# A hybrid decoder layer on one core: the output projection by token halves, the sample rows kept by channel through both norms, and the second norm's sums taken from accumulator outputs

## The reference, cut to what matters

```python
mix = (sigmoid(gate_pool) * A + sigmoid(gate_rwkv) * B) @ w_out
x  = LN1(ALPHA * x + (1 + gate1(c)) * mix)
h2 = LN0(x) * (1 + scale2(c)) + shift2(c)
ff = ConvFFN(h2)     # up-projection, causal conv of width 3, SiLU gate, down-projection
x  = LN2(ALPHA * x + (1 + gate2(c)) * ff)
```

## Time and profile before

| | |
|---|---|
| median of 3 runs | 1205.17 us (1204.91 to 1206.76) |
| the profiled execution | 1207.57 us, of it 1205.8 us from the first to the last instruction |
| PE busy | 1109.9 us, 92% |
| DVE, ACT, POOL busy | 58%, 40%, 8% |
| granted TensorE clock, mean | 0.977 of full |

### The profile page before, as it was taken

The page is one execution under the profiler, slowest core; times in us unless marked ns, Lnnn a source line. Parts: engine busy times, 40 slices in busy tenths (PEclk is TensorE's granted clock), DMA queues, the critical chain, the costliest instruction groups (busy, mean ns, idle before and its releaser), DMA issues.

```text
span 1205.8 us, 34828 instructions
## 1 busy us (share of the span) xinstructions
PE 1109.9 (92%) x15398; PEld 1028.4 (85%) x15398; DVE 705.3 (58%) x1141; ACT 484.5 (40%) x804; POOL 100.7 (8%) x152
## 2 busy tenths in 40 slices
PE   4789999999999999999989997799999989599995
PEld 2678888888888878999989997798999989599995
DVE  5456666677666663679316538756666576723336
ACT  2375344363443633543324233554443444413221
POOL 0003203032030310000000003100000000000000
PEclk9899999999999999999989999899999999899998
DMA  9502202102021102397775522322323223242221
GB/s 322 184 25 58 60 4 60 45 19 61 3 61 46 54 18 58 96 266 214 220 226 175 159 88 71 106 71 70 104 70 91 83 75 99 84 149 80 84 69 71
DMA packets 188225, 117.50 MB, mean 97 GB/s; under 512 B 6693, under 2 KB 180379, under 8 KB 187954
## 3 DMA queue, kind: packets, MB, share of 16 engines
q1 hardware_dynamic: 157333, 100.17, 27.7%
q10 hardware_dynamic: 30764, 15.40, 4.6%
HBM read 108.40 MB, written 7.34 MB: 96 GB/s over the span
## 4 chain that ended last, share of the span: by engine, by line
PE 30%; issue 8%; DVE 8%; ACT 7%; DMA 3%; SPq 1%; POOL 1%; DVEq 1%; ACTq 0%; POOLq 0%
PE PJ L231 22%; PE PJ L223 4%; ACT ACC L1938 2%; ACT Wh L1744 2%; DVE ACC L2338 2%; DVE ACC L2339 1%; DMA AD<-in_ada_w_dram 1%; DVE ACC L2346 1%; DVE ACC L2344 1%; ACT ACC L1936 1%; PE BB L1513 1%; DMA RAW<-in_w_in_dram 1%; DVE Wl L1988 1%; PE BB L231 1%; ACT SFh L1945 0%
## 5 line engine op out<-in xcount | busy, mean ns | idle before, releaser
L231 PE MATMUL PJ<-Hh,Wh 128*128 128x260 f32 (+1 forms) x1152 | 257.9, 305 | 20.2 <-DVE Wl L1988 13.6
L231 PE MATMUL PJ<-Hl,Wh 128*128 128x260 f32 (+1 forms) x1152 | 234.3, 285 | 0.0
L231 PE MATMUL PJ<-Hh,Wl 128*128 128x260 f32 (+1 forms) x1152 | 233.5, 284 | 0.0
L231 PEld LDWEIGHTS PJ<-Hh,Wh 128*128 128x128 f32 x1152 | 179.4, 190 | 43.5 <-issue 32.1
L1988 DVE TENSOR_TENSOR Wl<-RAW,Wh 128x1024 fp32r<-128x1024 f32 (+2 forms) x102 | 118.2, 1161 | 110.8 <-ACT Wh L1744 105.6
L231 PEld LDWEIGHTS PJ<-Hh,Wl 128*128 128x128 f32 x1152 | 180.0, 190 | 0.0
L231 PEld LDWEIGHTS PJ<-Hl,Wh 128*128 128x128 f32 x1152 | 179.6, 190 | 0.0
L1744 ACT ACTIVATE Wh<-RAW 128x1024 fp32r<-128x1024 f32 (+2 forms) x106 | 106.8, 1010 | 118.3 <-PE PJ L231 114.4
L2338 DVE SCALAR_TENSOR_TENSOR ACC<-ACC,CP 128x512 f32<-128x512 f32 x88 | 66.1, 751 | 72.7 <-ACT ACC L1938 71.1
L1304 POOL TENSOR_TENSOR MO<-BP,CST 128x512 f32<-128x512 f32 x40 | 55.9, 1405 | 309.4 <-DVE KP L1185 250.1
L231 PE MATMUL PJ<-SFh,Wh 128*128 128x256 f32 (+1 forms) x308 | 64.3, 290 | 13.4 <-DVE Wl L1988 13.4
(11 more groups left out here) (389 smaller groups left out, 2153.5 us busy)
## 6 DMA issues: line engine op xcount, KB each, us to landing
RAW<-in_w_in_dram SPq DMA_DIRECT2D x46, 512.0 KB, 5.3
RAW<-in_ffn_up_dram SPq DMA_DIRECT2D x44, 512.0 KB, 3.8
AD<-in_ada_w_dram ACTq DMA_DIRECT2D x19, 512.0 KB, 5.8
RAW<-in_ffn_down_dram SPq DMA_DIRECT2D x16, 512.0 KB, 3.9
RAW<-in_ada_w_dram ACTq DMA_DIRECT2D x10, 512.0 KB, 6.6
AW<-in_ada_w_dram SPq DMA_DIRECT2D x2, 2048.0 KB, 14.6
RAW<-in_w_branch_rwkv_dram SPq DMA_DIRECT2D x8, 512.0 KB, 4.1
RAW<-in_w_out_dram SPq DMA_DIRECT2D x8, 512.0 KB, 4.0
```

The source lines that it names most:

```text
L231: mm = pe.matmul(out[:, b, 0:nb[b]], w[:, slot, kw, :], x[:, kx, c0:c0 + nb[b]], start=first and w is Wh and x is xh, stop=last and w is Wl)
```

## The change

- **w_out by halves.** All eight blocks go by halves. First pass: tokens 256 to 519 of blocks 0 to 7 (`ohalf`, with `wt(e)` for the place of the split weights: blocks 4 to 7 lie in parts of `Hh` and `Hl`, so all eight stay). Second pass: tokens 0 to 255 in the order 4, 5, 0, 1, 2, 3, 6, 7. Tiles 2 and 3 are turned, added and normed during the second pass, turned back in it (`turn_x`), and the up-projection's first half is now tokens 256 to 519. Tiles 0 and 1 are normed during that.
- **Samples by channel.** The 8 sample columns are never turned to rows for a norm. They stay a 128x64 array (`XT_`, `GX`); `x_sample` is turned once to channels by PE; a norm's sums over channels are a `tensor_reduce` over the blocks on DVE and a small product with a matrix of 1/1024 on PE (`total`, `total2`), the root is ACT's (`root_s`). The weights and biases of both norms are loaded a second time by channel (four small loads on ACT's queue at the start). Only at the end PE turns the samples to rows for the output, and ACT copies them.
- **Sums from accumulators.** `stats_x` is gone. `finish_x` is `finish` with an accumulator output (the sum of the row); the mean's negative is one 128x1 operation; `root_x` is a `Square` over 128x1024 on ACT with an accumulator output and then the root.
- **No POOL between w_out and the up-projection.** The low parts of the four weight blocks and of `Hl` are made by DVE.
- **The end.** The last down block does tokens 256 to 519 first; tiles 2 and 3 are normed and stored before tiles 0 and 1. The sample rows' statistics, centring and finish are gone from DVE.

PE's queue, cut:

```diff
-                for e in range(NF):
+                for e in range(KT):
                     pe.wait_ge(S("w_lo"), B_OUT + e + 1)
+                    after(pe, "mo1", e - 1)
                     after(pe, "mo1_s", e - 1)
...
-                        mm = kstep(pe, PJ[e % 2], e % 4, k, MGh, MGl, k, k == 0, k == KT - 1, nh)
+                        mm = ohalf(PJ[e % 2][:, 0, 0:264], e, k, 256, 264)
+                    mm.then_inc(S("half"), 1)
+                    if e > 1 and e % 2 == 0:
+                        turn(e // 2 - 1, (e - 2, e - 1), (2, 3))
...
+                for p, e in enumerate(E2):
+                    after(pe, "mo1", KT + p - 1 if p > 1 else 0)
+                    for k in range(KT):
+                        if p == 0 and k == 3:
+                            turn(3, (6, 7), (2, 3))
+                        mm = ohalf(PJ[e % 2][:, 1, 0:256], e, k, 0, 256)
                     mm.then_inc(S("prj"), 1)
+                    if p == 0:
+                        total(0, 2)
+                    elif p == 1:
+                        total(1, 3)
+                    elif p == 2:
+                        turn(4, (4, 5), (0, 1))
+                    elif p == 3:
+                        total(2, 4)
+                    elif p == 4:
+                        turn(5, (0, 1), (0, 1))
+                        past(pe, "xn", 2)
...
+                        for b in range(3):
+                            turn_x(HA[b], b, (2, 3), b)
+                    elif p == 5:
+                        past(pe, "hfd", 1)
+                        turn_x(HA[3], 3, (2, 3), 3)
+                        total(3, 5)
+                    elif p == 6:
+                        turn(6, (2, 3), (0, 1))
+                turn(7, (6, 7), (0, 1))
```

DVE's and ACT's new norm steps, and POOL's part:

```diff
+                def finish_x(t, n):
+                    dve.scalar_tensor_tensor(x_row(t), x_row(t), RS1[:, t:t + 1], LNP[:, 1, :], ALU.mult, ALU.add,
+                                             accum_out=MVX[:, t, 0:1]).then_inc(S("x1"), 1)
+                    dve.wait_ge(S("x1"), n)
+                    dve.tensor_scalar(MVX[:, t, 1:2], MVX[:, t, 0:1], -1.0 / D, None, ALU.mult).then_inc(S("mv"), 1)
+                def s_centre(dst, mean, left, sq):
+                    dve.wait_ge(S("t_y"), left)
+                    need(mark(dve.tensor_tensor(dst, XT_, by_b(mean), ALU.subtract)))
+                    need(mark(dve.tensor_tensor(sq, dst, dst, ALU.mult)))
+                    dve.tensor_reduce(RED, over_k(sq), AX.X, ALU.add).then_inc(S("ys"), 1)
...
-                def root_x(t, n):
+                def root_x(t, n, left):
                     past(act, "mv", n)
+                    act.activation(xn_row(t), x_row(t), ACT.Square, bias=MVX[:, t, 1:2], accum_out=RS2[:, t:t + 1]).then_inc(S("sd"), 1)
+                    past(act, "sd", left)
+                    act.activation(RS2[:, t:t + 1], RS2[:, t:t + 1], ACT.Sqrt, bias=CST[:, C_EPS:C_EPS + 1], scale=1.0 / D).then_inc(S("sd"), 1)
...
-                for q in range(4):
-                    pool.wait_ge(S("w_hi"), B_FF + q + 1)
-                    pool.wait_ge(S("w_lo"), B_FF + q)
-                    pool.tensor_tensor(Wl[:, q], RAW[:, q], Wh[:, q].bitcast(F32), ALU.subtract).then_inc(S("w_lo"), 1)
-                for b in range(4):
-                    past(pool, "hh", b + 1)
-                    pool.tensor_tensor(Hl[:, 2 * b:2 * b + 2, 0:256], HR[:, 2 * (b % 2):2 * (b % 2) + 2, :],
-                                       Hh[:, 2 * b:2 * b + 2, 0:256].bitcast(F32), ALU.subtract).then_inc(S("hl_a"), 1)
```

More of the change, by code:

```diff
@@ L1878, in _ @@
+                gated1(0)
+                root(2, 4, 1)
+                gated1(1)
+                root_s(sums(1), 4)
+                root_x(2, 2, 2)
+                gated1(2)
+                normed(2, 1)
                 split_ff(0)
-                gated1(NF + 1)
+                root_x(3, 3, 4)
+                gated1(3)
+                normed(3, 2)
                 split_ff(1)
-                root_x(0, 2)
-                gated1(NF + 2)
+                gated1(4)
+                half_f(0, HA, 1)
@@ L1891, in _ @@
-                for b in range(4):
-                    after(act, "hl_a", b - 1)
-                    half_f(b, HA, b + 1)
-                    past(act, "hf", b + 1)
-                    half_h(b, 0)
-                    if b == 1:
-                        root(2, 5, 4)
-                root_x(2, 5)
-                normed(2, 3)
-                root_x(3, 6)
-                normed(3, 4)
-                root_x(4, 7)
+                act.wait_ge(S("hl_a"), 1)
+                half_f(2, HA, 3)
@@ L1903, in _ @@
+                past(act, "hf", 2)
+                half_h(2, 256)
+                gated1(6)
+                past(act, "hfd", 2)
+                act.activation(Hh[:, :, T:TN], HS, ACT.Copy).then_inc(S("hh"), 1)
+                past(act, "hfd", 3)
+                half_h(3, 256)
+                gated1(7)
+                root(0, 2, 4)
+                root_x(0, 5, 7)
+                normed(0, 3)
+                root_x(1, 6, 9)
+                normed(1, 4)
                 act.wait_ge(S("hl_a"), 3)
@@ new lines, in _ @@
+                dve.wait_ge(S("xa"), 4)
+                need(mark(chunk((2, 3), 3, x_row)))
+                joined((2, 3))
+                past(dve, "ld_c", 32)
+                past(dve, "mv", 1)
+                s_centre(XT_, sums(0), 3, GX)
+                c2 = centre(x_row, LNP, 2)
+                inverse(2, 4, 1)
+                need(c2)
+                finish_x(2, 1)
+                c3 = centre(x_row, LNP, 3)
+                inverse_x(2, 3)
+                need(c3)
+                finish_x(3, 2)
@@ new lines, in _ @@
+                joined((0, 1))
+                past(dve, "mv", 4)
+                c0 = centre(x_row, LNP, 0)
+                inverse(0, 2, 6)
+                need(c0)
+                finish_x(0, 3)
+                c1 = centre(x_row, LNP, 1)
+                inverse_x(0, 8)
+                need(c1)
+                finish_x(1, 4)
+                inverse_x(1, 10)
+                dve.wait_ge(S("hl_a"), 4)
+                half_f(1, HB, 6)
+                half_l(0, 6, 0, "hl_b")
+                half_l(1, 7, 0, "hl_b")
@@ L2365, in _, with add2 @@
                 J = TURNS1
-                def add2(e, tiles, sample):
-                    j = J + (e if e < KT - 1 or not sample else KT)
-                    add(j, XP2, XS2, tiles, e, 1, sample, B[2])
+                def add2(e, tiles):
+                    add(J + (e if e < KT - 1 or tiles[0] else KT), XP2, tiles, e, 1)
                 def lo_dn(e, q):
```

562 lines of the change are left out of this document (273 added, 289 removed).

## The result

The changed kernel takes 1185.59 us (median of 4 runs, 1183.3 to 1186.1), the kernel before beside it 1205.04 (4 runs, 1201.1 to 1206.76). The ratio is 0.9836, with a 95% interval of 0.9817 to 0.9855: 1.6% faster. The prediction said 1187.2 us, 1184 to 1194.5. The profiled execution took 1183.3 us, 1181.5 of it from the first to the last instruction.

The account below looks back on a forecast made before the run. PE, busy 92%, bounds the kernel; time comes only from its stops and low clock. `w_out` to loop: 76.8 work, 4.9 waits, 0.4 allowance, 82.1. Gains 16.0 + 0.7 + 1.3 = 18.0 give 1189.6 profiled, median 1187.2 us, range 1184 to 1194.5.

Parts of the forecast that it names:

- Work at full clock, 76.8: PE's work from `w_out` to the up-projection loop, in us: products, turns, sample transposes, sums, `XN` transposes, first four up blocks.
- First block, 0.9: First `w_out` block: a new PE wait of 0.9 us for the low part of `MGl` for `k = 7`.
- Tiles 2 and 3: no wait, margin 0.8: Second `w_out` pass: normed rows ready at 736.1 us, PE reaches them at 736.9; no wait.
- Tiles 0 and 1: a wait of 0.9: After the first up halves: PE ends at 760.3 us, `xn` 4 comes at 761.2, so PE waits 0.9.
- Accumulators, 0.2 each: Norm sums by accumulator output: 0.2 us each; rival: `finish_x` takes 1.2 more each, 1190.7 us, 10%.
- Second half, 1.3 and 1.0: Up blocks' second half: PE waits 1.3 us after transposing `XN`, then 1.0 for the third pair of blocks of `h2`.
- POOL's 7.6 us hidden: POOL's splits become 7.6 us of DVE work, covered by the second `w_out` pass; uncovered they would cost 7.6 us.
- The loads hidden: First loop weights: loads go at 758.6 us, ACT wants the first at 769.9, 3 us left; cost nothing.
- Down, 0.7 gained; last add 0.9 later: Down-projection: seven small transposes leave PE, 0.7 us gained; samples by channel move DVE's last add from 1193.5 to 1194.4.
- The end: After the last add: 3.4 us of sample work leaves DVE, last store lands about a microsecond later; 1.3 gained, 0.3 to 2.5.
- The low clock: Rival: clock falls again at PE's three waits between 760.3 and 768 us, costing 3 us; 1190.2 us, 17%.
- the slower rival's mechanism: DVE's 128x1 steps slow behind any large pass, not through POOL; 12 at 1.9 us each give 1210 us; 4%.

Follow-up runs that it names:

- The order that avoids it: Changed kernel with the last k of the first `w_out` block done after three k of the second block: 1185.85 us, ratio 0.9857; stretch 81.62.
- 2.2 in one piece, made on purpose: Changed kernel with six needless `bn_stats` ahead of the statistics of tiles 0 and 1: 1190.93 us, ratio 0.9885; stretch 85.40.
- the changed kernel again: Changed kernel run once more, unaltered, for a second profile: 1186.37 us, ratio 0.9853; stretch 82.60.
- the last: Changed kernel with first-block products reordered, last turn inside the first up block, tile 1's normed rows split between ScalarE and VectorE: 1185.72 us, ratio 0.9845.

## Why the prediction held, point by point

- **The bound.** Right: TensorE's stops for the norms, and the low clock behind them. With the stops the low clock went, 0.86 to 1.00 on the mean.
- **Work at full clock, 76.8.** Too low, and the largest error within the 82.1. In the chain `w_out`'s 384 matmuls sum to 47.0 us, not 45.5: 24 of them take 2.82 to 3.13 where 2.81 and 2.88 were put down. Turns, sums and sample transposes came to 3.74, 0.48 and 0.59 (3.6, 0.6, 0.7).
- **First block, 0.9.** Measured 0.75. The order that avoids it brought 1.0.
- **Tiles 2 and 3: no wait, margin 0.8.** Right: the normed rows are there 0.9 before TensorE wants them. What lay closer was not named: the samples' third sum, with 0.8.
- **Last eviction, 0.6.** Measured 0.57.
- **Tiles 0 and 1: a wait of 0.9.** There was none. From the start of `w_out` the last `XN` was due after 66.1 us and came after 66.4, so this chain was right. TensorE was due after 65.2 and came after 66.5, as its own work had been put too short. The error of 1.3 there took the place of the wait of 0.9.
- **Accumulators, 0.2 each.** VectorE's cost 0.08, ScalarE's 0.18, and `Square` took 1.15 where 1.24 was taken. `finish_x` did not pay in its rate: by the Trainium skill's rule (Vector Engine (DVE) Microarchitecture Reference, Points that are easy to get wrong) it should have halved, and the runs do not agree, at 1.28 us with the sum and 1.28 without.
- **Second half, 1.3 and 1.0.** The waits for `Hl` were 1.25 and 0.77. From its first transpose to the loop are 16.1 us, 0.4 more than the terms gave.
- **POOL's 7.6 us hidden.** Right: with the work on GpSimd or on VectorE the stretch is the same to 0.2. That without the cover of the second pass they would cost their 7.6 us is not what the old order shows: there VectorE's share of the work made TensorE wait 3.7 us, and the stretch fell by 1.9 all the same. That GpSimd slowed the small steps (2.0 us) was shown by taking it away: 0.157.
- **The loads hidden.** Right: issued at 751.58, and ScalarE's first split at 764.65 is released by TensorE.
- **Down, 0.7 gained; last add 0.9 later.** Together 0.2 later was forecast, 0.65 was measured. The six blocks after the first take 17.20 us each instead of 17.32, 0.7 less in all, as put down. But the first took 18.66 instead of 17.90 (start of the first product to the last of its 132), and there the clock is the cause. The stretches of 2 us below begin with the one that holds the first product, at 1054.58 in the kernel before and at 1031.94 in the one after; both have 13.4 us without work ahead of it.

```profile
1054.00:1056.00 2.00, 1.42 (x6) 1.45 (x7) 2.00 (x3) 0.85 (x2) 0.00 (x0) 0.50 0.12 36
1056.00:1058.00 2.00, 2.00 (x12) 2.00 (x12) 0.43 (x1) 0.00 (x0) 0.00 (x0) 0.61 0.83 248
1058.00:1060.00 2.00, 2.00 (x19) 2.00 (x18) 0.00 (x0) 0.00 (x0) 0.00 (x0) 1.00 0.96 273
```

```profile
1031.00:1033.00 2.00, 1.06 (x5) 1.09 (x6) 2.00 (x3) 1.22 (x2) 0.00 (x0) 0.50 0.04 12
1033.00:1035.00 2.00, 2.00 (x11) 2.00 (x11) 0.94 (x2) 0.00 (x0) 0.00 (x0) 0.50 0.99 289
1035.00:1037.00 2.00, 2.00 (x13) 2.00 (x13) 0.00 (x0) 0.00 (x0) 0.00 (x0) 0.60 0.98 283
1037.00:1039.00 2.00, 2.00 (x19) 2.00 (x18) 0.00 (x0) 0.00 (x0) 0.00 (x0) 1.00 1.02 307
```

- **The end.** 3.4 of VectorE was to go, and 3.1 went (9.97 to 6.85 us from the last add to the end of the last pass). The last store landed 3.1 us after its issue instead of 2.3: 0.8, against about one. The last add now follows at once behind the samples' affine step on VectorE: from TensorE's sum at 1164.7 on, VectorE alone sets the end.
- **The rivals.** The low clock did not come back: waits of 1.25 and 0.77 left it at 1.00, while 2.2 in one piece, made on purpose, brought 0.78 over five. That agrees with the Trainium skill (TensorE: Matmul & The Clock Gate, Part 1), by which idleness is what throttles. Small steps on VectorE take 0.15 to 0.28, so the slower rival's mechanism isn't there.

**The sum.** Predicted 18.0 off the profiled execution; 17.1 is found in the places it spoke of. The stretch came out within 0.5 us of its 82.1, and that is in part luck. TensorE's work took 79.0 us where 76.8 was put down, 2.2 more; its waits took 3.6 where 4.9 and an allowance of 0.4 were put down, 1.7 less. The two are not independent: work that lasts longer covers a wait, as with tiles 0 and 1. But nothing in the sum foresaw that.

The forecast of the median was 1.6 too high, since the timed difference is 19.4, 2.3 more than the 17.1. These 2.3 are not reproduced. The interval of the ratio is 17.5 to 22.1 us, its low end 0.4 above the 17.1, and the seven other timed runs of changed kernels, each beside the kernel before, don't show the rest. Their gain in time, 1205 us x (1 - ratio), lies between 0.9 less and 0.6 more than their gain in the stretch with 1.7 added for what follows the loop (2.31 - 0.65), 0.1 less on the mean: 17.7 against 17.1 for the changed kernel again, 14.5 against 14.8 without the accumulators, 18.7 against 18.6 for the last. The times do not bear out either that the changed kernels start `w_out` 2.5 us earlier. So the gain is about 17 us, in the places that the prediction named.

**What the gain is made of.** From the kernel before, leaving out the samples' way by rows is worth 6.2 us of the 15.5, GpSimd's part 1.9, both 7.3. The other 8.2 belong to the order by token halves with the accumulators, less what the samples by channel cost. Of these the accumulators are 2.4, measured in the new order. The order alone was not run; its 5.8 are a difference.

## What to carry to other kernels

Write down the matrix engine's work and waits in order, at full clock, and price an edit by the waits that it leaves: the sum came out within 0.5 us in 82, though single terms were off by up to 1.5 and it took opposite errors to get so near. Look at what a few odd rows cost on engines whose passes take as long for 8 rows as for 128, since they can stand in the chain as whole tiles. Removing one cause of a stop when others stand beside it may bring nothing: the same work off GpSimd gave 1.9 us and nothing timed in the old order, and 0.2 in the new.

## What the runs showed of the hardware

- How long the clock stays at 0.50 when work comes back differs, though the code around it and the wait ahead of it are the same. After the 13.4 us wait ahead of the down products, read in stretches of 1 us from the first product, it reached 1.00 in the fourth in both profiles of the kernel before, in the sixth in both of the changed kernel, and in the seventh in five others. What decides it is not shown. Two to three microseconds more at half the clock are 1 to 1.5 us of time.
- An accumulator's sum costs a separate small instruction: 0.08 us on VectorE, 0.18 to 0.19 on ScalarE.
- A two-input pass on GpSimd slows VectorE's 128x1 steps with two inputs in SBUF from 0.16 to 2.0 us if they meet. Not all steps: in the kernel before, a reciprocal of 128x1, with one input, took 0.15 us at 742.74, in the midst of GpSimd's splits, and the two-input step right behind it 2.08. GpSimd's own pass takes 2.4 to 2.9 us on the mean for the 1.22 of VectorE.
- `w_out`'s start varied by 7 us over 14 profiles of kernels with all but the same code ahead of it, with the waits for `in_ada_w` (0.8 to 5.0 us in sum, up to 2.5 for one) and with the clock, whose mean from 600 to 640 us was 0.91 to 1.00.
